# Layer norm between the blocks: statistics by tokens, and its mean at the end of the experts' stage

## The reference

```
def layer_norm(x, g, b):
    mu = x.mean(-1); var = square(x - mu).mean(-1)
    return (x - mu) * rsqrt(var + 1e-5) * g + b
...
x = layer_norm(alpha * x + gate * moe_ffn(h), ln2_g, ln2_b)   # end of the first block
h = rmsnorm(x, ffn1_norm)                                     # start of the second
x = x + 0.5 * swiglu(h, w_gate, w_up, w_down)
```

## Time and profile before

| | |
|---|---|
| Three runs | 2284.40, 2285.88, 2286.64 us; median 2285.88 |
| Profiled execution | 2287.78 us, of which the span of the program's instructions is 2286.0 |
| Granted TensorE clock, mean over the span | 0.975 |
| TensorE busy | 2158.6 us, 94% |
| Weight loads busy | 1486.5 us, 65% |
| VectorE busy | 1123.2 us, 49% |
| ScalarE busy | 774.7 us, 34% |

### The profile page before, as it was taken

One profiled execution on the slowest core, in us unless ns is written; L12 is line 12 of the kernel. 1 busy time (PEld: TensorE's weight loads), 2 busy tenths in 40 slices (PEclk: granted clock), 3 DMA queues, 4 the chain that ended last, 5 costly groups with the idle time before them and its releaser, 6 DMA issues. The chain is left out here.

```text
span 2286.0 us, 33281 instructions
## 1 busy us (share of the span) xinstructions
PE 2158.6 (94%) x13753; PEld 1486.5 (65%) x13753; DVE 1123.2 (49%) x1741; ACT 774.7 (34%) x1031; POOL 3.0 (0%) x6
## 2 busy tenths in 40 slices
PE   6978789999999999999997999999999999999999
PEld 5757644443333333333335889988888889988888
DVE  4764511111111111111116876778865875777874
ACT  3553311111111111001114554556544554546553
POOL 0000000000000000000000000000000000000000
PEclk9989999999999999999998999999999999999999
DMA  9443779999999999999985555434655655434552
GB/s 379 151 170 135 305 310 429 431 430 431 430 430 430 430 430 429 430 430 430 416 367 177 187 200 169 145 112 136 208 190 185 186 198 171 151 109 147 185 198 78
DMA packets 200228, 626.00 MB, mean 274 GB/s; under 512 B 13176, under 2 KB 150200, under 8 KB 164280
## 3 DMA queue, kind: packets, MB, share of 16 engines
q1 hardware_dynamic: 197512, 622.72, 70.6%
q10 hardware_dynamic: 2608, 1.72, 0.3%
HBM read 623.36 MB, written 1.05 MB: 273 GB/s over the span
## 5 line engine op out<-in xcount | busy, mean ns | idle before, releaser
L2067 DVE TENSOR_TENSOR w_low<-ring,w_high 128x2048 fp32r<-128x2048 f32 x168 | 384.0, 2290 | 173.1 <-ACT w_high L2062 173.1
L2062 ACT ACTIVATE w_high<-ring 128x2048 fp32r<-128x2048 f32 x168 | 320.7, 1910 | 182.1 <-PE bank L2407 141.4
L2402 PE MATMUL bank<-h_both,w_high 128*128 128x512 f32 x1344 | 322.5, 392 | 0.0
L1826 PE MATMUL bank<-ring,ut 128*64 128x512 f32 x1024 | 247.5, 634 | 36.8 <-DMA ring<-in_exp_w_dram 36.8
L2402 PEld LDWEIGHTS bank<-h_both,w_high 128*128 128x128 f32 x1344 | 246.7, 188 | 48.9
L1798 PE MATMUL bank<-ring_odd,xt 128*64 128x512 f32 x1024 | 224.4, 596 | 0.0
L1798 PE MATMUL bank<-ring,xt 128*64 128x512 f32 x1024 | 223.3, 594 | 0.3 <-ACT xt L1880 0.3
L1884 ACT ACTIVATE sg<-glu 128x512 f32<-128x512 f32 x32 | 20.2, 631 | 544.0 <-DVE glu L1947 544.0
L1826 PEld LDWEIGHTS bank<-ring,ut 128*64 128x64 f32 x1024 | 72.7, 144 | 195.8 <-issue 129.0
L1963 DVE SCALAR_TENSOR_TENSOR xT<-bank,mod,xT 128x256 f32<-128x256 f32 x128 | 55.6, 479 | 247.4 <-PE bank L1840 247.4
L2407 PEld LDWEIGHTS bank<-h_both,w_low 128*128 128x128 f32 x1344 | 167.5, 188 | 7.0
(11 more groups left out here) (552 smaller groups left out, 2704.7 us busy)
## 6 DMA issues: line engine op xcount, KB each, us to landing
ring<-in_exp_w_dram SPq DMA_DIRECT2D x64, 2048.0 KB, 26.9
ring_odd<-in_exp_w_dram SPq DMA_DIRECT2D x64, 2048.0 KB, 28.2
ring<-in_exp_w_dram SPq DMA_DIRECT2D x128, 1024.0 KB, 25.3
ring<-in_ffn_w_gate_dram SPq DMA_DIRECT2D x44, 1024.0 KB, 5.4
ring<-in_ffn_w_up_dram SPq DMA_DIRECT2D x44, 1024.0 KB, 5.4
ring<-in_ffn_w_down_dram SPq DMA_DIRECT2D x44, 1024.0 KB, 4.9
ring<-in_w_in_dram SPq DMA_DIRECT2D x36, 1024.0 KB, 5.4
ring<-in_ada_w_dram SPq DMA_DIRECT2D x24, 1024.0 KB, 12.5
```

What stands on the lines that cost most here:

```text
L1826: ins = nc.tensor.matmul(bank[2 + dh][64 * dh:64 * dh + 64, :], ut[:, r % 4, 64 * (r // 4):64 * (r // 4) + 64], w[:, x, 512 * dh:512 * dh ...
L2062: nc.scalar.activation(w_bufs[0][u % BUFS], ring2[:, u % RING2, :], ACT.Copy).then_inc(high2, 1)
L2067: nc.vector.tensor_tensor(w_bufs[1][u % BUFS], ring2[:, u % RING2, :], w_bufs[0][u % BUFS].bitcast(F32), ALU.subtract).then_inc(low2, 1)
L2402: return nc.tensor.matmul(b[:, :], w_parts[0][:, at:at + P], moving.rearrange("p a t -> p (a t)"), start=start, stop=False, skip_group_che ...
```

## The change

The mean is now made at the end of the experts' stage. Behind the last `back`, TensorE makes 16 one-column products with `xT` as the stationary operand (sums of 128 tokens x 2, bank 4); VectorE multiplies the identity matrix by each sum and -1/1024 (`mean_diag`, in a buffer of the stage that is free by then); TensorE multiplies ones with these diagonals, which spreads minus the mean of each token over all partitions of bank 5. The next stage reads it there.

In `opening` the two additions and the mean products are gone, and VectorE starts with the centering, now a plain addition. ScalarE starts with a square root on constants. The variance is made by 16 one-column products on the eight tiles of squares, without the pair additions. Root and reciprocal are taken of 128x2 numbers; VectorE makes two diagonals from them, TensorE spreads these over bank 7, and the scaling reads bank 7. `split_high(act, 0)` now stands behind the root.

```diff
@@ experts' stage, TensorE, behind back(LAST)
+                    for c in range(DC):
+                        if c % 2 == 0:
+                            pe.wait_ge(sem("acc_added"), 4 * LAST + c // 2 + 1)
+                        for a in range(TT):
+                            ins = nc.tensor.matmul(bank[4][:, a:a + 1], xT[:, c, P * a:P * a + P], ones[:, 0:1], start=(c == 0 and a == 0),
+                                                   stop=(c == DC - 1), skip_group_check=True)
+                    ins.then_inc(sem("x_sums"), 1)
+                    pe.wait_ge(sem("mean_diagonal"), 1)
+                    for a in range(TT):
+                        nc.tensor.matmul(bank[5][:, P * a:P * a + P], ones, mean_diag[:, a, :], start=True, stop=True)
@@ experts' stage, VectorE, behind the last add_back
+                    dve.wait_ge(sem("x_sums"), 1)
+                    for a in range(TT):
+                        ins = nc.vector.tensor_scalar(mean_diag[:, a, :], ident, bank[4][:, a:a + 1], -1.0 / D, ALU.mult, ALU.mult)
+                    ins.then_inc(sem("mean_diagonal"), 1)
@@ opening, TensorE
-                pe.wait_ge(sem("halves_added"), 2)
-                for c in range(2):
-                    ins = nc.tensor.matmul(mean, ones, halves[:, c, :], start=(c == 0), stop=(c == 1))
-                ins.then_inc(sem("mean_ready"), 1)
-                for c in range(4):
-                    pe.wait_ge(sem("pairs_added"), c // 2 + 1)
-                    ins = nc.tensor.matmul(var, ones, squares[:, 4 * (c // 2) + c % 2, :], start=(c == 0), stop=(c == 3))
+                for c in range(DC):
+                    if c % 2 == 0:
+                        pe.wait_ge(sem("squares"), c // 2 + 1)
+                    for a in range(TT):
+                        ins = nc.tensor.matmul(square_sums[:, a:a + 1], squares[:, c, P * a:P * a + P], ones[:, 0:1], start=(c == 0 and a == 0),
+                                               stop=(c == DC - 1), skip_group_check=True)
                 ins.then_inc(sem("var_ready"), 1)
+                pe.wait_ge(sem("root_diagonal"), 1)
+                for a in range(TT):
+                    ins = nc.tensor.matmul(spread[:, P * a:P * a + P], ones, root_diag[:, a, :], start=True, stop=True)
+                ins.then_inc(sem("rstd_spread"), 1)
@@ opening, ScalarE
+                nc.scalar.activation(r_tok[:, :], ones[:, 0:TT], ACT.Sqrt)
                 for j in range(4):
                     act.wait_ge(sem("centered"), j + 1)
                     nc.scalar.activation(squares[:, 2 * j:2 * j + 2, :], xT[:, 2 * j:2 * j + 2, :], ACT.Square).then_inc(sem("squares"), 1)
+                act.wait_ge(sem("var_ready"), 1)
+                nc.scalar.activation(r_tok[:, :], square_sums, ACT.Sqrt, bias=1e-5, scale=1.0 / D).then_inc(sem("root_ready"), 1)
                 split_high(act, 0)
-                act.wait_ge(sem("var_ready"), 1)
-                nc.scalar.activation(root[:, :], var, ACT.Sqrt, bias=1e-5, scale=1.0 / D).then_inc(sem("root_ready"), 1)
@@ opening, VectorE
-                st.step(nc.vector.tensor_tensor(halves, xT[:, 0:4, :], xT[:, 4:8, :], ALU.add), "halves_added")
-                st.step(nc.vector.tensor_tensor(halves[:, 0:2, :], halves[:, 0:2, :], halves[:, 2:4, :], ALU.add), "halves_added")
+                for j in range(4):
+                    xj = xT[:, 2 * j:2 * j + 2, :]
+                    st.tell(nc.vector.tensor_tensor(xj, minus_mean.unsqueeze(1).to_broadcast([P, 2, T]), xj, ALU.add), "centered")
...
-                dve.wait_ge(sem("mean_ready"), 1)
-                for j in range(4):
-                    st.tell(nc.vector.scalar_tensor_tensor(xj, mean.unsqueeze(1).to_broadcast([P, 2, T]), -1.0 / D, xj, ALU.mult, ALU.add), "centered")
-                for k in range(2):
-                    dve.wait_ge(sem("squares"), 2 * k + 2)
-                    st.tell(nc.vector.tensor_tensor(squares[:, 4 * k:4 * k + 2, :], ...), "pairs_added")
                 dve.wait_ge(sem("root_ready"), 1)
-                st.step(nc.vector.reciprocal(root[:, :], root[:, :]))
+                st.step(nc.vector.reciprocal(r_tok[:, :], r_tok[:, :]))
+                for a in range(TT):
+                    ins = nc.vector.tensor_scalar(root_diag[:, a, :], ident, r_tok[:, a:a + 1], None, ALU.mult)
+                st.step(ins, "root_diagonal")
+                dve.wait_ge(sem("rstd_spread"), 1)
                 for j in range(4):
-                    st.tell(nc.vector.tensor_tensor(xj, xj, root[:, :].unsqueeze(1).to_broadcast([P, 2, T]), ALU.mult), "scaled")
+                    st.tell(nc.vector.tensor_tensor(xj, spread.unsqueeze(1).to_broadcast([P, 2, T]), xj, ALU.mult), "scaled")
```

More of the change, by code:

```diff
@@ L1715, in build @@
             y = sb("y", [P, D], where=c8)
+            mean_diag = glu[:, 0:T].rearrange("p (a t) -> p a t", a=TT)
             with nc.Fori(0, n_passes) as p, Stage(nc, pool) as S:
@@ L2192, in opening @@
             sem = S.sem
-            mean, var = bank[6][:, 0:T], bank[7][:, 0:T]
-            halves = qp[:, :, :]
+            minus_mean, square_sums, spread = bank[5][:, 0:T], bank[6][:, 0:TT], bank[7][:, 0:T]
+            root_diag = root[:, :].rearrange("p (a t) -> p a t", a=TT)
             def tensor(pe):
-                pe.wait_ge(sem("halves_added"), 2)
-                for c in range(2):
-                    ins = nc.tensor.matmul(mean, ones, halves[:, c, :], start=(c == 0), stop=(c == 1))
-                ins.then_inc(sem("mean_ready"), 1)
-                for c in range(4):
-                    pe.wait_ge(sem("pairs_added"), c // 2 + 1)
-                    ins = nc.tensor.matmul(var, ones, squares[:, 4 * (c // 2) + c % 2, :], start=(c == 0), stop=(c == 3))
+                for c in range(DC):
[4 more added lines that the diff above has]
+                                               stop=(c == DC - 1), skip_group_check=True)
                 ins.then_inc(sem("var_ready"), 1)
+                pe.wait_ge(sem("root_diagonal"), 1)
+                for a in range(TT):
+                    ins = nc.tensor.matmul(spread[:, P * a:P * a + P], ones, root_diag[:, a, :], start=True, stop=True)
+                ins.then_inc(sem("rstd_spread"), 1)
             def scalar(act):
+                nc.scalar.activation(r_tok[:, :], ones[:, 0:TT], ACT.Sqrt)
                 for j in range(4):
@@ L2228, in vector @@
                 st.tell(nc.vector.memset(fox_bias[:, :], 0.0), "bias_cleared")
-                st.step(nc.vector.tensor_tensor(halves, xT[:, 0:4, :], xT[:, 4:8, :], ALU.add), "halves_added")
-                st.step(nc.vector.tensor_tensor(halves[:, 0:2, :], halves[:, 0:2, :], halves[:, 2:4, :], ALU.add), "halves_added")
+                for j in range(4):
+                    xj = xT[:, 2 * j:2 * j + 2, :]
+                    st.tell(nc.vector.tensor_tensor(xj, minus_mean.unsqueeze(1).to_broadcast([P, 2, T]), xj, ALU.add), "centered")
                 for k, name in enumerate(("ln2_g", "ln2_b")):
                     nc.vector.tensor_tensor(open_gain[:, k, :], par(name, 0, DC), par("ffn1_norm_2", 0, DC), ALU.mult)
-                dve.wait_ge(sem("mean_ready"), 1)
+                dve.wait_ge(sem("root_ready"), 1)
+                st.step(nc.vector.reciprocal(r_tok[:, :], r_tok[:, :]))
[3 more added lines that the diff above has]
+                dve.wait_ge(sem("rstd_spread"), 1)
                 for j in range(4):
                     xj = xT[:, 2 * j:2 * j + 2, :]
-                    st.tell(nc.vector.scalar_tensor_tensor(xj, mean.unsqueeze(1).to_broadcast([P, 2, T]), -1.0 / D, xj, ALU.mult, ALU.add), "centered")
-                for k in range(2):
-                    dve.wait_ge(sem("squares"), 2 * k + 2)
-                    st.tell(nc.vector.tensor_tensor(squares[:, 4 * k:4 * k + 2, :], squares[:, 4 * k:4 * k + 2, :], squares[:, 4 * k + 2:4 * k + 4, :],
-                                                    ALU.add), "pairs_added")
-                dve.wait_ge(sem("root_ready"), 1)
-                st.step(nc.vector.reciprocal(root[:, :], root[:, :]))
-                for j in range(4):
-                    xj = xT[:, 2 * j:2 * j + 2, :]
-                    st.tell(nc.vector.tensor_tensor(xj, xj, root[:, :].unsqueeze(1).to_broadcast([P, 2, T]), ALU.mult), "scaled")
+                    st.tell(nc.vector.tensor_tensor(xj, spread.unsqueeze(1).to_broadcast([P, 2, T]), xj, ALU.mult), "scaled")
                     if j == 1:
```

## The result

| | before | after |
|---|---|---|
| Median of 20 runs, us | 2286.50 (2283.16 to 2291.74) | 2289.84 (2285.41 to 2293.25) |
| Ratio, 95% interval | 1 | 1.0015 (1.0008 to 1.0021) |
| Profiled execution, us | 2287.78 | 2291.72 |

The change makes the kernel slower by 0.15%, between 1.8 and 4.8 us. The forecast was 2288.4 us, 2.5 over the median before, with 81% on a difference that 0.2% does not separate. The median after is 1.4 over the forecast, of which 0.6 is that the median of 20 runs before lies above that of the three runs the forecast started from. The interval is narrower than 0.2% because 20 runs on each side stand behind it; a single pair of runs would not have shown the difference, since the runs of one kernel spread over 8 us.

What follows compares the result with a forecast made beforehand. The prediction saw TensorE busy for 94% of the span, with the edit inside a 26 us handover mostly at low clock. +3.3 at the scaling less 0.8 gives +2.5; 2287.78 + 2.5, less 1.90, is 2288.4 us, range 2282.3 to 2292.0.

Steps and rivals of the forecast that it cites:

- Mean: End of the experts' stage to centering: removed and added work cost the same, between -0.6 and +0.5 us; +0.5 taken.
- Table load: Start of the next stage on ScalarE: loading the square root's table ahead of the first square costs 0.8 us.
- Square sums: Variance on TensorE: 32 instructions of one-column products at the low clock, spaced by 0.222 us, take 7.4 us.
- the stated bounds: Spacing of the square sums' loads at the low clock: 0.111 us (no growth) to 0.337 us (no overlap).
- rivals one and three: First: square sums keep 0.111 us each, 2283.9 us, chance 0.26; third: their loads don't overlap at low clock, 2292.1, 0.12.
- Rival two: Square sums keep 0.111 us each and the first weight unit also runs at full clock: -4.65, 2281.2 us, chance 0.07.
- Root: From variance to scaling: root, reciprocal, two diagonals, spread and hops take 2.4 us, against 2.24 before.
- Loads of the next stage: Transfers behind the barrier move from 1213.8 to about 1218.3; the first unit's later split covers its landing at 1223.7.
- First unit: First weight unit dense 3.3 us later; 0.8 us given back through the clock's rise, half of 1.65.
- the second case: First weight unit: the clock rises at the same moment as before, 1238.5, and 1.65 us come back.
- What is lost or won here moves the end by the same amount: After the 26 us seam TensorE runs without gaps, so any change there shifts the kernel's end equally.
- Sum: Whole edit: +3.3 us at the scaling less 0.8 in the first unit, +2.5; 2288.4 us, chance 0.52.

Runs made afterwards that it cites:

- e3: e1 with unit 0's split moved behind the root and an early root on constants bringing the table; scaling at 14.73 us after the last addition, no ratio.
- e2: Kernel before with only the new variance (one-column sums, early root on constants, diagonals and spread), mean as before; ratio 1.0006.
- e5: Changed kernel with the root on constants, and so the table load, behind the four squares on ScalarE; ratio 1.0010.
- e4: Changed kernel with 60 unread products ahead of the square sums, and those sums made four times over; loads 0.112 us at full clock, 0.213 at half.
- e6: Changed kernel with VectorE's pair additions kept, so 8 one-column products instead of 16 make the variance; ratio 0.9999.
- e1: Changed kernel with variance, root and order of the split put back as before, only the mean made in the experts' stage; ratio 1.0008.
- e8: Kernel before with the mean made in the experts' stage by 8 wide products, split behind the root, early root on constants; ratio 0.9993.
- e9: e8 with products read by nobody where TensorE waits in the seam; ratio 0.9987.
- e7: Kernel before with products of ones with the identity, read by nobody, where TensorE waits in the seam; ratio 0.9988.

## Why the prediction was right, step by step

- *Mean: +0.5 forecast, +0.28 measured.* The train took 3.94 us for 3.74 to 4.1 forecast (it began 0.4 before the last back product ended, and the last loads ran at the low clock, which fell 2.2 after the last addition, at 1216.5). Diagonals 0.49 for 0.6, spread 1.22 for 1.3. The barrier took 0.98 from the end of the spread at 1218.89 to VectorE's first instruction at 1219.87, as the earlier trace rows said for VectorE arriving last. e3 puts the step at 0.25.
- *Table load: 0.8 forecast, 0.57 measured* (e2 against the change, and e5). The first square was ready 2.0 after the stage's start instead of 2.15.
- *Square sums: 7.4 forecast, 6.99 measured.* The chosen value of 0.222 per load was near; it is 0.213 at the low clock (e4, e6). Both ends of the stated bounds, 0.111 and 0.337, were wrong for this place, and with them rivals one and three; half the columns made 2.3 us at the scaling (e6). Rival two fell with the first, since the changed kernel had no full-clock moment from 1216.5 to 1240.4.
- *Root: 2.4 forecast; 2.31 measured*, from the end of the sums at 1228.85 to 1231.16.
- *Loads of the next stage: covered, as forecast.* The changed kernel issues the first unit at 1219.82, 5.5 after the last addition and 4.4 later than before; it landed 5.4 later, at 1225.2, and the split came at 1228.95. e1 also shows what the early table load is for: with split and table load both ahead of the root, the late transfer costs 1.4. In the changed kernel the square sums end so late that the split was covered in either place, by its rows.
- *First unit: 0.8 given back forecast, 1.0 in this pair of executions.* Of the prediction's two cases the second came out: the clock rose 26.1 us after the last addition, before 26.0. In e1, e2, e3 and e5 it rose 25.4 to 26.5 after it, in e6 and e8 at 23.6 and 22.7; counted from the first dense product it was anything from 3.4 (e6) to 6.1 us (e3). What sets the moment one execution of each doesn't show. The forecast took half of the second case's 1.65 for want of a reason. That this came near 1.0 is luck: the shift it was half of was 2.4 and not 3.3.
- *"What is lost or won here moves the end by the same amount": not shown by this pair, and wrong for a large gain.* The second unit came 1.36 later and the last instruction 2.3; the 0.9 between them arose behind the seam and has no term in the forecast. In e9, 2.7 of the 6.1 us won at the second unit were gone at the end.
- *Sum.* +3.3 forecast at the scaling, +2.40 measured, the terms being 0.2, 0.2, 0.4 and 0.1 too large; +2.5 in all, against +1.36 at the second unit and +2.3 at the last instruction of this pair, and +3.3 between the medians. The mechanism is the one forecast, a train of 32 loads at the low clock between the squares and the root. That +2.5 in all comes so near +2.3 is in part luck: the terms were 0.9 too large at the scaling, and 0.9 arose where the forecast had nothing. What separates the traces from the median difference of 3.3 is not shown and lies within the interval.

## What to carry to other kernels

A product with one moving column is not cheap in time: it costs its weight load, 0.112 us per f32 instruction at full clock and 0.213 at half here, and in this seam most of them were paid at half. Count the loads, not the columns, and compare with wide products that leave the sum already spread. When work is put ahead of a barrier, look at what the barrier releases: here the first weight transfer moved with it, and an order of split, table load and root that was harmless before became 1.4 us (e1). And before speeding up a short handover, see who is next: with 6.1 us won in the seam, 1.3 went to a wait for VectorE at the third unit.

## What the runs showed of the hardware

One-column products kept TensorE busy for 22.3 us at a granted clock of 0.50 without a rise, after they had begun at 1.00 (e4). In the same execution the 128x128 products ahead of them had begun at 0.50 (at 1217.0) and ran at 1.00 from 1221.5 on. Such products, read by nobody, in the waits of the seam kept the clock at 1.00 all through it (e9) and made the kernel before 0.12% faster by themselves (e7, 0.03 to 0.21%). That useless work in idle time pays is the surprise here: the prediction had the low clock as a price of the added products, and not as a price that the kernel before was already paying for its own.
